# Output projection of a hybrid mLSTM and pooling block: tokens instead of channels on the partitions

## What is computed

```python
def _merge(parts, y_m, y_p, out_w):
    g_m, g_p = jnp.split(parts['g_branch'], 2, axis=-1)
    return (jax.nn.sigmoid(g_m) * y_m + jax.nn.sigmoid(g_p) * y_p) @ out_w

x = x + gate * _merge(parts_x, y_m, y_p, out_w)     # gate: one value a channel
return _rmsnorm(x, final_norm_w)                    # over the 1024 channels of a token
```

## Time and profile before

| | us |
|---|---|
| median of 3 runs | 2506.68 |
| lowest, highest | 2505.91, 2507.99 |
| the profiled execution, its own time | 2509.72 |
| its span, first to last instruction | 2507.9 |
| TensorE busy with products | 2395.1 |
| TensorE busy with weight loads (beside products) | 2002.5 |
| VectorE, ScalarE, GpSimd busy | 1204.9, 787.8, 315.7 |

### The profile page before, as it was taken

The page is one execution under the profiler, slowest core; times in us unless marked ns, Lnnn a source line. Parts: engine busy times, 40 slices in busy tenths (PEclk is TensorE's granted clock), DMA queues, the critical chain, the costliest instruction groups (busy, mean ns, idle before and its releaser), DMA issues. The chain is left out here.

```text
span 2507.9 us, 34424 instructions
## 1 busy us (share of the span) xinstructions
PE 2395.1 (96%) x12267; PEld 2002.5 (80%) x12267; DVE 1204.9 (48%) x2340; ACT 787.8 (31%) x1625; POOL 315.7 (13%) x323
## 2 busy tenths in 40 slices
PE   7899999999999999999999999999999589999997
PEld 5667888888888878888888878888888478777775
DVE  2612212222222224566666756676666465656472
ACT  2521111111111112334433334343434335353532
POOL 1011000000000002122112111321120112020200
PEclk9999999999999999999999999999999799999998
DMA  8337324434423437767676698666766556656562
GB/s 244 128 78 258 120 98 122 126 94 121 135 93 120 128 84 228 221 224 228 198 233 232 216 319 228 227 220 205 221 223 231 179 161 200 213 192 217 186 216 70
DMA packets 464482, 453.61 MB, mean 181 GB/s; under 512 B 24012, under 2 KB 405604, under 8 KB 462780
## 3 DMA queue, kind: packets, MB, share of 16 engines
q1 hardware_dynamic: 423628, 386.69, 48.8%
q10 hardware_dynamic: 33296, 33.56, 5.1%
q0 software_dynamic: 7392, 31.15, 3.3%
HBM read 311.25 MB, written 140.05 MB: 180 GB/s over the span
## 5 line engine op out<-in xcount | busy, mean ns | idle before, releaser
L1198 PE MATMUL bank<-xlate,wh 128*128 128x512 f32 x2048 | 673.6, 403 | 10.9 <-DVE v_t L1328 4.9
L1198 PEld LDWEIGHTS bank<-xlate,wh 128*128 128x128 f32 x2048 | 375.0, 190 | 81.2 <-DVE v_t L1328 5.3
L1198 PE MATMUL bank<-xlate,wl 128*128 128x512 f32 x1024 | 410.9, 401 | 0.0
L625 PE MATMUL bank<-xearly,wh 128*128 128x512 f32 (+1 forms) x1280 | 367.3, 372 | 0.0
L625 PE MATMUL bank<-xlate,wh 128*128 128x512 f32 x1024 | 322.1, 396 | 0.0
L625 PEld LDWEIGHTS bank<-xearly,wh 128*128 128x128 f32 x1280 | 228.4, 188 | 39.0
L625 PE MATMUL bank<-xearly,wl 128*128 128x512 f32 (+1 forms) x640 | 236.6, 370 | 0.0
L625 PEld LDWEIGHTS bank<-xlate,wh 128*128 128x128 f32 x1024 | 191.1, 189 | 39.2
L1198 PEld LDWEIGHTS bank<-xlate,wl 128*128 128x128 f32 x1024 | 194.4, 190 | 34.4
L625 PE MATMUL bank<-xlate,wl 128*128 128x512 f32 x512 | 201.4, 393 | 0.0
L831 DVE SCALAR_TENSOR_TENSOR qks<-bank,qks 128x512 fp32r<-128x512 f32 (+1 forms) x72 | 47.5, 661 | 299.3 <-ACT qks L701 299.3
(11 more groups left out here) (249 smaller groups left out, 4216.2 us busy)
## 6 DMA issues: line engine op xcount, KB each, us to landing
v_t<-vk_d SPq DMA_DIRECT2D x144, 384.0 KB, 4.1
qk_d<-qks SPq DMA_DIRECT2D x64, 512.0 KB, 2.7
q_t<-qk_d SPq DMA_DIRECT2D x128, 256.0 KB, 5.3
wraw<-in_in_w_dram ACTq DMA_DIRECT2D x31, 1024.0 KB, 12.6
wraw<-in_in_w_dram SPq DMA_DIRECT2D x32, 512.0 KB, 7.7
vk_d<-vs SPq DMA_DIRECT2D x64, 256.0 KB, 2.8
k_t<-qk_d SPq DMA_DIRECT2D x64, 256.0 KB, 5.9
wraw<-in_branch_m_w_dram SPq DMA_DIRECT2D x32, 512.0 KB, 4.0
```

The source lines that it names most:

```text
L625: mm = pe.matmul(bank[m % 4][:, 0:w], a[:, u % 2, k, :], xn(b, k, t0, w), start=(k == 0 and n == 0), stop=(k == KT - 1 and n == 2))
L1198: mm = pe.matmul(bank[m % 2][:, :], a[:, u % 2, k, :], xlate[part][:, k, tq * TQ:(tq + 1) * TQ], start=(k == 0 and n == 0), stop=(k == KT ...
```

## The change

The output unit makes its product with the operands in each other's place. A 128 x 128 slice of m_h or m_l (128 channels by 128 tokens) is stationary and the 128 columns of the weight tile move, so that a product gives 128 tokens by 128 channels, with tokens on the partitions. Each unit does this for four token tiles, which go to the four quarters of a bank: 96 products of 128 columns in place of 24 of 512. The transposes and ScalarE's copy go away. The gate now varies along the row, so it is written to memory once in the second stage (by gpsimd's queue, one element at a time), and loaded as a row over all partitions (`gate_row`, 512 KB) behind `fn_row`. VectorE's residual becomes two operations: PSUM times gate row into `og`, then `og` plus `xo`.

Unit 0 of a block goes over k outermost for the first three token tiles, in banks 0, 6 and 7, since its operand becomes ready k by k; the fourth follows. The very last unit of all goes token tile by token tile into four banks, with a semaphore for each, and residual, squares, statistics, norm and store follow for each token tile by itself.

```diff
+                pool.dma_start(gate_d.rearrange("j p -> p j"), mgate[:, :],
+                               allow_slow_non_contiguous=True).then_inc(gate_stored, 16)
                 pool.wait_ge(xe_stored, 32)
+                pool.wait_ge(gate_stored, 16)
...
                 sp.dma_start(fn_row[:, :], final_norm_w.partition_broadcast(P)).then_inc(rows_loaded[2], 16)
+                sp.dma_start(gate_row[:, :], gate_d.rearrange("j p -> (j p)").partition_broadcast(P)).then_inc(rows_loaded[3], 16)
...
+            FIRST = [bank[0], bank[6], bank[7], bank[0]]
+            LAST = [bank[1], bank[6], bank[7], bank[2]]
...
                 def output_unit(i, n):
...
-                    products(bank[n % 2], weight(i * NT5 + T_O + n), (m_h, m_l), 0, KT, ready)
+                    w = weight(i * NT5 + T_O + n)
+                    def part(dst, k, q):
+                        at = slice(q * P, (q + 1) * P)
+                        for r, (a, c) in enumerate(((m_h, 0), (m_h, 1), (m_l, 0))):
+                            mm = pe.matmul(dst[:, at], a[:, k, at], w[c][:, k, :],
+                                           start=(k == 0 and r == 0), stop=(k == KT - 1 and r == 2))
+                        return mm
+                    last = (i, n) == (NTQ - 1, KT - 1)
+                    rest, dst = range(QT), LAST if last else [bank[n % 2]] * QT
+                    if n == 0:
+                        for k in range(KT):
+                            pe.wait_ge(m_hi, i * KT + k + 1)
+                            pe.wait_ge(m_lo, i * KT + k + 1)
+                            for q in range(QT - 1):
+                                part(FIRST[q], k, q)
+                        rest = range(QT - 1, QT)
+                    for q in rest:
+                        for k in range(KT):
+                            mm = part(dst[q], k, q)
+                        if last:
+                            mm.then_inc(tail_done, 1)
+                    if not last:
+                        mm.then_inc(unit_done, 1)
-                def turn_output(i, n):
-                    pe.wait_ge(of_made, i * KT + n + 1)
...
-                def output(i, n):
...
-                    act.activation(of[:, n % 2], bank[n % 2][:, :], ACT.Copy,
-                                   scale=mgate[:, n:n + 1]).then_inc(of_made, 1)
...
                 def residual(i, n):
+                    c = i * KT + n
+                    dve.wait_ge(unit_done, i * NU + 2 * KT + n + 1)
                     s = slice(n * P, (n + 1) * P)
...
+                    if n == 0:
+                        for q in range(QT):
+                            read = dve.tensor_tensor(og[:, q, :], FIRST[q][:, q * P:(q + 1) * P], gate_row[:, s], ALU.mult)
+                        read.then_inc(o_read, 1)
+                    else:
+                        dve.tensor_tensor(og[:, :, :], bank[n % 2][:, :].rearrange("p (q f) -> p q f", f=P),
+                                          gate_row[:, s].unsqueeze(1).broadcast_to([P, QT, P]), ALU.mult).then_inc(o_read, 1)
...
+                    dve.wait_ge(o_read, c + 1)
+                    dve.tensor_tensor(xo[:, :, s], og[:, :, :], xo[:, :, s], ALU.add).then_inc(x_added, 1)
...
+                def tail_residual(q):
+                    c, s = NTQ * KT - 1 + q, slice(D - P, D)
+                    dve.wait_ge(tail_done, q + 1)
...
+                    dve.tensor_tensor(og[:, q, :], LAST[q][:, q * P:(q + 1) * P], gate_row[:, s],
+                                      ALU.mult).then_inc(o_read, 1)
+                    dve.wait_ge(o_read, c + 1)
+                    dve.tensor_tensor(xo[:, q, s], og[:, q, :], xo[:, q, s], ALU.add).then_inc(x_added, 1)
...
                 i = NTQ - 1
-                residual(i, KT - 2)
-                residual(i, KT - 1)
-                out_stats(i)
+                tail_residual(0)
                 for q in range(QT):
+                    if q + 1 < QT:
+                        tail_residual(q + 1)
+                    tail_stats(q)
                     out_norm(i, q)
```

More of the change, by code:

```diff
@@ L1583, in hybrid_block @@
             m_l = sb("m_l", [P, KT, TQ], FP32R)
-            of = sb("of", [P, 2, TQ])
+            og = sb("og", [P, QT, P])
+            gate_row = sb("gate_row", [P, D])
             xo = sb("xo", [P, QT, D])
@@ L1593, in hybrid_block @@
             unit_done = sem("unit_done")
-            rows_loaded = [sem(f"rows_loaded{n}") for n in range(3)]; rows_ready = sem("rows_ready")
+            rows_loaded = [sem(f"rows_loaded{n}") for n in range(4)]; rows_ready = sem("rows_ready")
             pw_hi = sem("pw_hi"); pw_lo = sem("pw_lo")
@@ L1910, in merged_hi @@
                     act.activation(m_h[:, n], mm_[:, :], ACT.Copy).then_inc(m_hi, 1)
-                def output(i, n):
-                    act.wait_ge(unit_done, i * NU + 2 * KT + n + 1)
-                    if i * KT + n >= 2:
-                        act.wait_ge(o_turned, i * KT + n - 1)
-                    act.activation(of[:, n % 2], bank[n % 2][:, :], ACT.Copy,
-                                   scale=mgate[:, n:n + 1]).then_inc(of_made, 1)
                 def out_square(i, part, q):
-                    act.wait_ge(x_added, i * KT + (KT - 1, KT)[part])
+                    tail = q if part and i == NTQ - 1 else 0
+                    act.wait_ge(x_added, i * KT + (KT - 1, KT)[part] + tail)
                     c = i * (2 * QT + 1) + part * QT + q
@@ L1946, in _ @@
                         T = i * NT5 + t
-                        if i and t == 0:
-                            output(i - 1, KT - 1)
                         if T + 2 < NTQ * NT5:
@@ L1985, in _ @@
                     out_square(i, 0, q)
-                output(i, KT - 1)
+                out_square(i, 1, 0)
                 for q in range(QT):
-                    out_square(i, 1, q)
-                out_root(i)
+                    if q + 1 < QT:
+                        out_square(i, 1, q + 1)
+                    tail_root(q)
             @block.vector
@@ new lines, in tail_stats @@
+                def tail_stats(q):
+                    c = (NTQ - 1) * 3 + 3 * q
+                    dve.wait_ge(o_act, (NTQ - 1) * (2 * QT + 1) + QT + q + 1)
+                    dve.tensor_tensor(oss[:, 3, q:q + 1], oss[:, 0, q:q + 1], oss[:, 0, QT + q:QT + q + 1],
+                                      ALU.add).then_inc(o_dve, 1)
+                    dve.wait_ge(o_dve, c + 1)
+                    dve.tensor_scalar(oss[:, 1, q:q + 1], oss[:, 3, q:q + 1], 1.0 / D, EPS, ALU.mult, ALU.add).then_inc(o_dve, 1)
+                    dve.wait_ge(tail_act, q + 1)
+                    dve.reciprocal(oss[:, 3, QT + q:QT + q + 1], oss[:, 2, q:q + 1]).then_inc(o_dve, 1)
+                    dve.wait_ge(o_dve, c + 3)
@@ L2094, in _ @@
                         T = i * NT5 + t
-                        if i and t == 0:
-                            residual(i - 1, KT - 2)
                         if T + 2 < NTQ * NT5:
@@ L2127, in _ @@
                             n = t - T_O
-                            if n >= 2:
-                                residual(i, n - 2)
+                            if n >= 1:
+                                residual(i, n - 1)
                             if i + 1 < NTQ:
```

39 lines of the change are left out of this document (16 added, 23 removed).

## The result

The changed kernel takes 2668.6 us (median of 4 runs, 2667.2 to 2670.4), where the kernel before took 2507.3 us beside it (4 runs, 2505.9 to 2509.9). The ratio is 1.064, with a 95% interval of 1.062 to 1.066: 161 us slower. The forecast was 2646 us with a range of 2622 to 2680; the direction and most of the size are right, and 23 us are missing from the sum. The profiled execution took 2667.2 us, its span is 2665.4 us (2507.9 before), the mean granted clock 0.986 (0.983 before).

A forecast was written before the change was run, and what follows sets the result against it. TensorE was taken as the bound, busy 2395.1 of 2507.9 us. 341.0 - 175.2 - 13.2 (transposes) - 2.8 - 1.5 (waits) + 0.5 (gate row) - 9.7 (end) = +139.1 us, giving 2646 us, range 2622 to 2680.

The forecast's parts named there:

- Price of a narrow product: Output units: 0.111 us per 128-column product, 96 a unit, so 341.0 us in place of 175.2 us over 32 units.
- Shared loads: Rival, output units: two products with the same m_h slice share a load; 114 us less, 2532 us; chance 0.06.
- bare columns: Rival, output units: loads overlap fully, only 58 ns of columns left per product; 163 us less, 2483 us; chance 0.03.
- The clock: Rival, output units: granted clock falls to 1.2 GHz; 341 us more, 2987 us; chance 0.05.
- Supply of instructions within a unit: Rival: 192 TensorE instructions a unit instead of 56 cause a stop of about 1 us each; 2678 us; chance 0.04.
- Waits: Output stages of blocks 1 and 2: TensorE's 1.5 and 1.3 us waits for the next block's pooled inputs vanish, -2.8 us.
- pooled waits: Early pooled part of blocks: TensorE's 3 x 2.4 us without products shrinks by 1.5 us (bounds 0 and 7.1).
- VectorE at nothing: Output units: the two-operation residual adds 0.69 us a unit, 22 us in all, costing nothing on the path.
- The end: After the last product: 9.5 us instead of 19.2, a gain of 9.7 us (bounds 8 and 10.7).
- the case in which VectorE is not behind: Kernel's end: if VectorE keeps up with TensorE's token tiles, 8.5 us after the last product instead of 9.5.
- The store of 1024 single elements ... so 0: Second stage, gpsimd's queue: the gate's store costs 0, since nothing there needs it for hundreds of microseconds.
- The load of the row itself: Start, SP's queue behind fn_row: the 512 KB gate row load costs 0.5 us, at most 2.9 us.

The follow-up runs named there:

- narrow128: Kernel before, weights still stationary, with each 512-column product of 28 output units cut into four of 128 columns: 2667.6 us, ratio 1.062.
- narrow256: Kernel before, weights still stationary, with each 512-column product of 28 output units cut into two of 256 columns: 2540.4 us, ratio 1.012.
- pe_pad: Kernel before with 2000 small 32 x 32 products on TensorE behind everything else: 2613.6 us, ratio 1.042.
- store_only: Kernel before plus only the gate tensor, its store of 1024 single elements and the wait for it: 2521.4 us, ratio 1.004.
- no_gate_store: Changed kernel without the gate tensor and its store, gate row loaded from the final norm's weights: 2668.1 us, ratio 1.062 against the kernel before.
- wide_swap: Against the kernel before: tokens on partitions, 512 weight columns moving, gate row made on chip, last two units tile by tile: 2496.9 us, ratio 0.995.

## Why the prediction came out as it did

- **Price of a narrow product: right.** 0.111 us, from the earlier trace rows, measured 0.111 to 0.112 (10.67 / 96, 85.7 / 768) in the output units of the changed kernel and 0.111 in those of narrow128. What is left of the stretch's +151.3 us when the change of the waits (-2.2) is taken out is +153.5 us for products and transposes, against 152.6 in the forecast. The Trainium skill ("TensorE: Matmul & The Clock Gate", section "Back-to-back issue gap") has 81 ns for a pair at 128 columns and 131 ns at 512; the runs disagree, with 111 and 228. Its section "LDWEIGHTS (loading the stationary operand)" has columns / 1.2, 107 ns for 128 columns, and the 111 measured lie near it.
- **Shared loads and bare columns: wrong as rivals.** The loads are as many as the products. narrow256 and narrow128 show a floor: half the columns cost 0.120 instead of 0.228 us, a quarter of them 0.111. pe_pad shows that the floor is not a price of each pair as such: 0.053 us with 32 columns.
- **The clock: wrong as a rival.** The granted clock is 1.00, at 2.4 GHz, in all output stages. (Under the 32-column products of pe_pad it was 0.50.)
- **Supply of instructions within a unit: wrong as a rival.** No gap stands in an output stage.
- **Waits.** The 2.8 us in the output stages went, as forecast. The pooled waits didn't fall by 1.5 us: they grew from 7.1 to 7.7. That step is off by 2.1 us.
- **VectorE at nothing: right.** Its two operations take 0.68 and 0.77 us on 512 columns, no product waits for them, and VectorE is busy for 34 of 86 us.
- **The end: right, slightly undersized.** 8.1 us instead of 9.5, below the 8.5 of the case in which VectorE is not behind: of the last tile, residual starts 0.3 us after the last product in place of 1.0.
- **"The store of 1024 single elements ... so 0": this is the step that failed.** I looked for who needs the stored gate, and nobody does. I didn't look at what shares the way with it: neighbouring stores, whose buffers ScalarE and VectorE then wait for. It costs 7.3 us in the changed kernel and 11.3 in store_only, and no_gate_store gets it back. The load of the row itself can hardly have cost more than the 0.5 us allowed: the last stage up to the first hidden unit grew by 1.2 us, and wide_swap, without it, has 72.1 us there against 72.0.
- **A term that was missing altogether:** the scan, +11.3 us. The forecast counted only stages that the diff touches. The runs show that with a longer TensorE program the packets of the scan's weight queue take 1.4 to 1.7 times as long, and that the scan is 7 to 25 us longer; the cause behind it is not shown.
- **The range: held partly by luck.** Without the margin for a product's price its upper end was 2646 + 5.6 = 2651 us. The price needed none of its 28 us; they covered a loss in stages for which the range had no term. (Its terms add up to 2621 and 2679; it was stated as 2622 to 2680.)

The account in us, with products and transposes as the remainder: forecast 139.1, products and transposes +0.9, waits +2.1, the end -1.4, everything ahead of the first hidden unit +16.8 (17.3 instead of 0.5), together 157.5, the difference of the two spans.

## What to carry to other kernels

Before swapping the operands of a product, count loads, and not columns: here a load of 128 stationary columns with its product takes 0.111 us or more, and the load is hidden only behind a product of about 256 columns or more, so keep the wide dimension moving and change the tiling of the weights instead (wide_swap has the same layout for 172 us less). A store of single elements can have a price even where nobody waits for it, as the 7 to 11 us here; price it by the transfers beside it, or make the row on the chip. And cut both spans at the same events after a change: a loss may lie in a stage whose code is the same.

## What the hardware showed that I had not expected

- A DMA of 4 KB as 1024 elements of 4 bytes landed 33.5 to 35.6 us after its issue, and beside it the core's DMA throughput fell from 228 to some 155 GB/s at a higher busy share.
- Packets of ScalarE's queue took 1.4 to 1.7 times their time when TensorE's program was 1344 to 4352 instructions longer, in a stage hundreds of microseconds before those instructions, and not with 1400 more on ScalarE.
- 2000 products of 32 columns, each with a load of 32, ran 0.053 us apart without a gap for 107 us, behind a wait of 5.8 us, and the granted clock was 0.50 all the while (pe_pad, 2502.1 to 2609.4 us).
- The recorded length of a narrow product depends on its neighbours (223 ns between wide ones, 274 among narrow ones, 0.111 us apart); only the distance from start to start can be summed.
